# Last stage of an encoder block: the product with p split into high and low parts, and two even row tiles loaded earlier

## What is computed

```python
r = DEEPNORM_ALPHA * h + moe_ffn(h, ...)                       # 512 x 1024
r = r + jax.nn.sigmoid(r @ ple_w_gate[i]) * (p[i] @ ple_w_proj[i])   # p: 512 x 256
h = layer_norm(r, ln2_g[i], ln2_b[i])
```

## Time and profile before

| | us |
|---|---|
| median of 3 runs | 1092.02 |
| lowest and highest | 1091.96, 1093.88 |
| the profiled execution | 1090.4 |
| its span, first to last instruction | 1088.6 |
| TensorE busy | 1059.9 (97%) |
| VectorE busy | 853.4 (78%) |
| ScalarE busy | 716.7 (66%) |
| mean granted TensorE clock | 0.997 |

### The profile page before, as it was taken

One profiled execution on the slowest core, in us unless ns is written; L12 is line 12 of the kernel. 1 busy time (PEld: TensorE's weight loads), 2 busy tenths in 40 slices (PEclk: granted clock), 3 DMA queues, 4 the chain that ended last, 5 costly groups with the idle time before them and its releaser, 6 DMA issues.

```text
span 1088.6 us, 15813 instructions
## 1 busy us (share of the span) xinstructions
PE 1059.9 (97%) x5382; PEld 864.9 (79%) x5382; DVE 853.4 (78%) x906; ACT 716.7 (66%) x819; POOL 237.1 (22%) x173
## 2 busy tenths in 40 slices
PE   5999999999999999999999999999999999999996
PEld 4778877778888767888888888888888888888585
DVE  6654345663355788999999999999999999999476
ACT  3431244451242527888889988888998888888643
POOL 1000000000005120333333333333333333332101
PEclk9999999999999999999999999999999999999998
DMA  8532221214356449999999999999999999999831
GB/s 296 196 117 78 78 78 39 79 39 155 116 199 237 155 133 347 366 388 391 384 379 384 392 372 392 395 389 388 382 385 374 392 385 390 382 390 342 271 120 61
DMA packets 72571, 294.80 MB, mean 271 GB/s; under 512 B 15312, under 2 KB 18384, under 8 KB 47696
## 3 DMA queue, kind: packets, MB, share of 16 engines
q1 hardware_dynamic: 52944, 256.43, 60.0%
q0 software_dynamic: 19008, 35.71, 12.7%
q10 hardware_dynamic: 576, 2.10, 0.5%
HBM read 283.67 MB, written 44.04 MB: 301 GB/s over the span
## 4 chain that ended last, share of the span: by engine, by line
PE 92%; DMA 3%; DVE 2%; ACT 1%; issue 1%; SPq 0%; DVEq 0%; POOLq 0%; ACTq 0%
PE ps L416 26%; PE ps L418 25%; PE ps L417 25%; PE ps L1562 5%; PE ps L1586 1%; PE ps L1275 1%; PE ps L753 1%; PE ps L777 1%; PE ps L764 1%; DMA residual_rows<-y,put_idx 1%; DMA raw<-in_w_in 1%; DVE w_lo L400 1%; PE ps L325 1%; ACT w_hi L395 1%; PE ps L1546 0%
## 5 line engine op out<-in xcount | busy, mean ns | idle before, releaser
L1825 DVE TENSOR_TENSOR w_lo<-gu_raw,w_hi 128x2048 fp32r<-128x2048 f32 x128 | 292.3, 2284 | 1.0 <-ACT w_hi L1673 1.0
L1673 ACT ACTIVATE w_hi<-gu_raw 128x2048 fp32r<-128x2048 f32 x128 | 245.0, 1916 | 0.0
L416 PE MATMUL ps<-w_hi,xgT_hi 128*128 128x512 f32 x512 | 200.1, 391 | 0.8 <-issue 0.8
L418 PE MATMUL ps<-w_hi,xgT_lo 128*128 128x512 f32 x512 | 199.8, 390 | 0.0
L417 PE MATMUL ps<-w_lo,xgT_hi 128*128 128x512 f32 x512 | 199.2, 389 | 0.0
L1830 DVE TENSOR_TENSOR dn_lo<-dn_raw,dn_hi 128x2048 fp32r<-128x2048 f32 x62 | 142.2, 2293 | 20.8 <-ACT dn_hi L1682 20.8
L416 PE MATMUL ps<-w_hi,act_hi 128*128 128x512 f32 x368 | 146.6, 398 | 0.0
L418 PE MATMUL ps<-w_hi,act_lo 128*128 128x512 f32 x368 | 143.7, 390 | 0.0
L417 PE MATMUL ps<-w_lo,act_hi 128*128 128x512 f32 x368 | 143.4, 390 | 0.0
L1682 ACT ACTIVATE dn_hi<-dn_raw 128x2048 fp32r<-128x2048 f32 x62 | 118.8, 1917 | 0.0
L416 PEld LDWEIGHTS ps<-w_hi,xgT_hi 128*128 128x128 f32 x512 | 96.1, 188 | 21.3 <-issue 1.3
(11 more groups left out here) (218 smaller groups left out, 1763.6 us busy)
## 6 DMA issues: line engine op xcount, KB each, us to landing
gu_raw<-in_moe_w_gate SPq DMA_DIRECT2D x64, 1024.0 KB
gu_raw<-in_moe_w_up SPq DMA_DIRECT2D x64, 1024.0 KB
dn_raw<-in_moe_w_down SPq DMA_DIRECT2D x62, 1024.0 KB
raw<-in_w_in SPq DMA_DIRECT2D x18, 1024.0 KB, 5.2
h_rows<-x_rows SPq DMA_DIRECT2D x8, 512.0 KB, 4.5
raw<-in_w_out SPq DMA_DIRECT2D x4, 1024.0 KB, 4.9
ple_raw<-in_ple_w_gate SPq DMA_DIRECT2D x4, 1024.0 KB, 9.9
x_rows<-in_x SPq DMA_DIRECT2D x4, 512.0 KB, 10.0
```

Source lines behind the costliest of these rows:

```text
L416: nc.tensor.matmul(out, x_hi, w_hi, start=first, stop=False)
L418: return nc.tensor.matmul(out, x_lo, w_hi, start=False, stop=last)
L1673: nc.scalar.activation(m.w_hi[:, 2 * x.b + half], m.gu_raw[:, 2 * x.b + half], ACT.Copy).then_inc(gu_hi, 1)
L1825: nc.vector.tensor_tensor(m.w_lo[:, 2 * x.b + half], m.gu_raw[:, 2 * x.b + half], m.w_hi[:, 2 * x.b + half].bitcast(F32), ALU.subtract).th ...
```

## The change

- p times its weights is made with `product3` from high and low parts: `p_w_hi` (ScalarE, `split_p_weights`), `p_w_lo` and `pT_lo` (VectorE, `low_p`), `pT_hi` (ScalarE, `copy_turned_p`, which wrote `pT` before). In the last expert ScalarE does `split_p_weights` and `copy_turned_p` ahead of `scale_y` of expert 62; VectorE does `low_p` after `split_hT(63)`.
- The eight units go to banks 2, 7, 5, 6, 0, 1, 2, 7. Unit 0 waits for the first half of `pT_lo`, unit 4 for the second. `turn(0)` stands after all eight units.
- SP waits for the last scatter into `residual_rows` and loads the even rows of tiles 0 and 1; after `scattered` it loads the odd rows of tiles 0 and 1, gate weights 3, then tiles 2 and 3. The gains of the last norm are loaded once all eight units are summed.
- On ScalarE `copy_pp(0)` stands ahead of `split_hi(0)`, and the other copies move up in the same way. On VectorE `split_lo(3)` and `add_rows(1)` change places.

```diff
-        self.pT = at("pT", [P, 2, SEQ], F32, 188)
+        self.pT_hi = at("pT_hi", [P, 2, SEQ], F32R, 188)
+        self.pT_lo = at("pT_lo", [P, 2, SEQ], F32R, 184)
+        self.p_w_hi = at("p_w_hi", [P, HC], F32R, 168)
+        self.p_w_lo = at("p_w_lo", [P, HC], F32R, 192)
...
                 embedding.load_weights(sp, 2)
+                sp.wait_ge(put[0], 16 * ((r + 1) * (NE // 2) + ZEROS[0]))
+                embedding.load_even(sp, 0)
+                embedding.load_even(sp, 1)
...
                     split_hT(x)
+                    with act.If(peak[0] <= (x.r + 1) * CAP):
+                        embedding.split_p_weights(act)
+                        embedding.copy_turned_p(act)
                     scale_y(x.next(-1))
                     put_list(x)
-                    with act.If(peak[0] <= (x.r + 1) * CAP):
-                        embedding.copy_turned_p(act)
                     scale_y(x, bank=XT)
...
                     split_down(x, -1)
                     split_hT(x)
+                    with dve.If(peak[0] <= (x.r + 1) * CAP):
+                        embedding.low_p(dve)
...
+    OUT = (2, 7, 5, 6, 0, 1, 2, 7)
...
+    def load_even(self, sp, t):
+        sp.dma_start(self.m.x[:, t], self.acc[0][t * P:(t + 1) * P, :]).then_inc(self.rows_in[t], 16)
+
+    def load_odd(self, sp, t):
+        sp.dma_start(self.m.x_odd[t // 2][:, t % 2], self.acc[1][t * P:(t + 1) * P, :]).then_inc(self.rows_in[t], 16)
...
         sp.wait_ge(self.scattered, 1)
-        for t in range(NT):
-            sp.dma_start(m.x[:, t], self.acc[0][t * P:(t + 1) * P, :]).then_inc(self.rows_in[t], 16)
-            sp.dma_start(m.x_odd[t // 2][:, t % 2], self.acc[1][t * P:(t + 1) * P, :]).then_inc(self.rows_in[t], 16)
-            if t == 0:
-                self.load_weights(sp, 3)
+        self.load_odd(sp, 0)
+        self.load_odd(sp, 1)
+        self.load_weights(sp, 3)
+        for t in range(2, NT):
+            self.load_even(sp, t)
+            self.load_odd(sp, t)
+        sp.wait_ge(self.p_sum, 2 * NT)
         self.norm.load_affine(sp, self.a["ln2_g"][0], self.a["ln2_b"][0])
...
+    def split_p_weights(self, act):
+        act.wait_ge(self.pw_in, 16)
+        self.nc.scalar.activation(self.m.p_w_hi[:], self.m.p_w[:], ACT.Copy).then_inc(self.pw_hi, 1)
+
+    def low_p(self, dve):
+        m = self.m
+        dve.wait_ge(self.pw_hi, 1)
+        self.nc.vector.tensor_tensor(m.p_w_lo[:], m.p_w[:], m.p_w_hi[:].bitcast(F32), ALU.subtract).then_inc(self.pw_lo, 1)
+        for pair, bank in enumerate(self.PT):
+            cols = slice(2 * pair * P, 2 * (pair + 1) * P)
+            dve.wait_ge(self.pT_hi_done, 2)
+            self.nc.vector.tensor_tensor(m.pT_lo[:, :, cols], self.turned_p(bank), m.pT_hi[:, :, cols].bitcast(F32),
+                                         ALU.subtract).then_inc(self.pT_ready, 1)
...
-        pe.wait_ge(self.pw_in, 16)
+        pe.wait_ge(self.pw_lo, 1)
         for u in range(2 * NT):
             t, c = divmod(u, 2)
-            if u == 0:
-                pe.wait_ge(self.pT_ready, 2)
-            if u >= 2:
-                pe.wait_ge(self.p_out, u - 1)
+            if u in (0, 4):
+                pe.wait_ge(self.pT_ready, u // 4 + 1)
+            if u == 2:
+                pe.wait_ge(self.p_out, 1)
+            if u >= 6:
+                pe.wait_ge(self.p_out, u - 5)
             for j in range(2):
-                last = nc.tensor.matmul(ps[:, MAIN[c]], m.pT[:, j, t * P:(t + 1) * P],
-                                        m.p_w[:, j * D + c * 512:j * D + (c + 1) * 512],
-                                        start=(j == 0), stop=(j == 1))
+                rows, cols = slice(t * P, (t + 1) * P), slice(j * D + c * 512, j * D + (c + 1) * 512)
+                last = product3(nc, ps[:, self.OUT[u]], m.pT_hi[:, j, rows], m.pT_lo[:, j, rows],
+                                m.p_w_hi[:, cols], m.p_w_lo[:, cols], j == 0, j == 1)
             last.then_inc(self.p_sum, 1)
-            if u == 6:
-                turn(0)
+        turn(0)
...
+        copy_pp(0)
         ring.split_hi(act, 0)
-        copy_pp(0)
+        copy_pp(1)
         ring.split_hi(act, 1)
-        copy_pp(1)
         copy_pp(2)
+        copy_pp(3)
         ring.split_hi(act, 2)
-        copy_pp(3)
-        copy_pp(4)
-        copy_pp(5)
-        copy_pp(6)
+        for u in range(4, 2 * NT):
+            copy_pp(u)
         high_part(0)
-        copy_pp(7)
         ring.split_hi(act, 3)
...
         low_part(0)
+        ring.split_lo(dve, 3)
         add_rows(1)
-        ring.split_lo(dve, 3)
```

More of the change, by code:

```diff
@@ L2002, in __init__ @@
         self.p_turned, self.pT_ready, self.p_sum, self.p_out = sem("p_turned"), sem("pT_ready"), sem("p_sum"), sem("p_out")
+        self.pw_hi, self.pw_lo, self.pT_hi_done = sem("pw_hi"), sem("pw_lo"), sem("pT_hi_done")
         self.row_sum, self.turned, self.hi_done, self.lo_done = (sem("row_sum"), sem("turned"), sem("hi_done"),
@@ L2025, in load_weights @@
         self.ring.load(sp, i)
+    def load_even(self, sp, t):
+        sp.dma_start(self.m.x[:, t], self.acc[0][t * P:(t + 1) * P, :]).then_inc(self.rows_in[t], 16)
+    def load_odd(self, sp, t):
+        sp.dma_start(self.m.x_odd[t // 2][:, t % 2], self.acc[1][t * P:(t + 1) * P, :]).then_inc(self.rows_in[t], 16)
     def sync(self, sp):
-        m = self.m
         sp.wait_ge(self.scattered, 1)
-        for t in range(NT):
-            sp.dma_start(m.x[:, t], self.acc[0][t * P:(t + 1) * P, :]).then_inc(self.rows_in[t], 16)
-            sp.dma_start(m.x_odd[t // 2][:, t % 2], self.acc[1][t * P:(t + 1) * P, :]).then_inc(self.rows_in[t], 16)
-            if t == 0:
-                self.load_weights(sp, 3)
+        self.load_odd(sp, 0)
[5 more added lines that the diff above has]
+        sp.wait_ge(self.p_sum, 2 * NT)
         self.norm.load_affine(sp, self.a["ln2_g"][0], self.a["ln2_b"][0])
@@ L2053, in copy_turned_p, with turned_p @@
             act.wait_ge(self.p_turned, pair + 1)
-            self.nc.scalar.activation(self.m.pT[:, :, 2 * pair * P:2 * (pair + 1) * P],
-                                      self.ps[:, bank].rearrange("p (j n) -> p j n", n=2 * P),
-                                      ACT.Copy).then_inc(self.pT_ready, 1)
+            self.nc.scalar.activation(self.m.pT_hi[:, :, 2 * pair * P:2 * (pair + 1) * P], self.turned_p(bank),
+                                      ACT.Copy).then_inc(self.pT_hi_done, 1)
+    def turned_p(self, bank):
+        return self.ps[:, bank].rearrange("p (j n) -> p j n", n=2 * P)
+    def split_p_weights(self, act):
[10 more added lines that the diff above has]
+                                         ALU.subtract).then_inc(self.pT_ready, 1)
     def gpsimd(self, pool):
@@ L2092, in tensor @@
             if u < 2:
-                pe.wait_ge(self.p_out, 2 * NT - 1 + u)
+                pe.wait_ge(self.p_out, 5 + u)
             else:
@@ L2131, in copy_pp @@
             act.wait_ge(self.p_sum, u + 1)
-            nc.scalar.activation(m.pp[:, t, c * 512:(c + 1) * 512], ps[:, self.MAIN[c]],
+            nc.scalar.activation(m.pp[:, t, c * 512:(c + 1) * 512], ps[:, self.OUT[u]],
                                  ACT.Copy).then_inc(self.p_out, 1)
```

## The result

| | before | changed |
|---|---|---|
| median, us | 1091.99 (6 runs) | 1095.84 (6 runs) |
| lowest and highest | 1090.94, 1093.88 | 1094.73, 1096.76 |
| profiled execution, us | 1090.4 | 1095.33 |
| its span | 1088.6 | 1093.5 |
| mean granted clock over the runs | 0.9972 (beside the experiments) | 0.9947 |

The ratio is 1.0038, with a 95% interval of 1.0028 to 1.0048: 3.8 us slower (the interval is 3.1 to 5.2 us), where 1.6 were forecast. The time lies 0.3 us above the stated range.

A forecast was written before the change was run, and what follows sets the result against it. Bound by the chain from expert 63 through the last scatter and row loads to turn(0), tied with TensorE's p products. turn(0) 0.4 us late, less 0.3, then the swap's hold: turn(1) +1.6, median 1093.6, range 1091.6 to 1095.5.

The forecast's parts named there:

- The p product's 3.5 us: TensorE's products with p: 48 matmuls in 10.9 us instead of 14.4, 3.5 us less work but not on the path.
- the tie at turn(0): Before turn(0), two paths tie: the seventh p product ends at 1029.65 us, tile 0's rows are there at 1029.76.
- ScalarE's order: New copies ahead of scale_y(62) on ScalarE start it 1.55 us later and make the last scatter 1.1 us later.
- the gap of 0.30 on GpSimd: Between scatters 62 and 63 on GpSimd: 0.30 us taken, starting scatter 63 at 1019.8; with 0.72, 1020.2.
- The way from turn(0) to the end of gate unit 0: On TensorE, without unit 7's passes after the turn: 8.05 us instead of 8.35, giving back 0.3.
- the row loads: Early even loads: first takes 3.6 us, odd 0 lands at 1028.9, turn(0) only 0.4 us later than before.
- rival B: Gate weights 3 land later still, at 1035.9 with a 9.9 us load; turn(1) ends 3.5 us late, 1095.5; chance 0.25.
- the swap: split_lo(3) ahead of add_rows(1) on VectorE: TensorE waits from 1038.25 to 1039.45, turn(1) ends 1.6 us later.
- Rival A: turn(1) is not held, gate weights 3 landing by 1032.8; +0.1 to +0.4 us left, median 1092.3; chance 0.2.
- the clock at no charge: TensorE's new idle pieces of 1.5, 1.1, 1.1 and 1.2 us are too short to lower the clock; nothing charged.
- Rival D: Clock falls in the 1.5 us gap before the p products; 48 half-speed matmuls take 10.9 us more, 1102 at worst; chance 0.03.

The follow-up runs named there:

- e11: Changed kernel with old load order, swap undone, VectorE making p_w_hi, expert 62's rows scaled first, two idle pieces filled: 1091.65 us, ratio 0.9999 to the kernel before.
- e2: Changed kernel with the row loads in the old order, none issued before all scatters are done: 1093.36 us, ratio 1.0021 to the kernel before.
- e5: Changed kernel with old load order, weights of p loaded earlier and split in ScalarE's idle time, turned p copied behind put_list(63): 1092.5 us, ratio 1.0008.
- e1: Changed kernel with only VectorE's swap undone, add_rows(1) ahead of split_lo(3) again: 1095.23 us, ratio 1.0036 to the kernel before.
- e3: Changed kernel with eight extra matmuls, results overwritten, filling TensorE's wait for the first half of pT_lo: 1095.79 us, ratio 1.0048 to the kernel before.
- c1: The changed kernel itself measured and profiled once more, nothing altered: 1096.2 us, ratio 1.0035 to the kernel before.
- e6: As e5, with VectorE's swap undone and only tile 0's even rows loaded after scatter 62: 1093.67 us, ratio 1.0024 to the kernel before.

## Why the prediction was wrong, point by point

**Right: the direction and where to look.** The p product's 3.5 us were not on the path (e11: 0.9999), the tie at turn(0) was real, and ScalarE's order was what moved the scatters. That step stands nearly to the number: scatter 63 at D + 3.07 forecast, D + 3.48 and D + 2.92 in the two profiles, with the gap of 0.30 on GpSimd that I took over 0.72. Alone it costs 1.6 us. I had it at 1.1 at the scatter, and then let the early loads pay it back. The way from turn(0) to the end of gate unit 0 took 8.04 us, as forecast (8.05). But the direction came out right in part by luck: the term that made most of my 1.6 us is worth 0.2.

**Wrong, the largest step: the row loads.** I gave the first early load 3.6 us, the time of one with nothing ahead, let the queue run on at the old pace, and had odd 0 land at D + 12.2, 3.9 us after its issue. The early loads were issued about when I had them (D + 6.4 against D + 6.0), but they hardly moved before the last scatter had landed, and the first took 6.0 us. Odd 0 followed behind both at the pace of my sum and landed at D + 14.9, 6.3 us after its issue, and 6.8 in the second profile. In the old order only one load stands ahead of it, and turn(0) comes 1.3 us sooner (e2). The prediction weighed that the even loads share the engines with the last scatter, but only as an argument for rival B. Early loads are a cost and not a repayment: +1.2 us on the kernel before, 0.7 with the clock held up. Gate weights 3 stood behind them: 9.36 us where I had 8, which is near rival B's 9.9. Rival B named a load that was late, and its sum (1095.5) came out near in part by luck: its path is the one through the swap, which costs 0.2, and the clock is not in it. Rival A's estimate had gate weights 3 down at 1031.9, which is D + 15.2; they landed at D + 18.9.

**Wrong: what holds turn(1).** I made the swap the main term, 1.2 us of waiting. It would have held, had turn(0) not been 2.7 us later than I put it; as it was, both paths arrived within 0.1 us, and undoing the swap gives 0.2 with the clock held up and without. A wait that the chain names last is no price: the path beside it has to be read too.

**Wrong: the clock at no charge.** I compared idle pieces of 1.1 to 1.5 us one by one with a single row, 3.9 us of idleness at the end (the last matmul ended at 1079.0, the clock fell at about 1082.9). Here the clock fell after 1.92 us in one profile and while TensorE idled for 3.34 in another, and over all runs its mean fell by 0.0025. Rival D had the place (the gap ahead of the first product) at a chance of 0.03 and was priced as one large loss. In truth the mean was 0.993 to 0.996 in all twelve executions of the changed kernel (0.996 to 0.998 before), so the clock falls in most or all of them. Among the products of the changed kernel this costs nothing, since they still end 1.5 us ahead of turn(0) (in e5, where the rows came sooner, it cost 0.5). Where it meets gate unit 0, the way from turn(0) to turn(1) is 2.3 to 3.4 us longer (e1, e3, c1). On average over the runs the clock costs 1.1 to 1.4. The Trainium skill, "TensorE: Matmul & The Clock Gate", section on HAM oscillation, says that waits between bursts of matmuls send the clock back to half; the waits of its example are longer, about 3 to 5 us. These runs show the same behind shorter ones: the mean went from 0.9947 to 0.9975 when the idle pieces were filled.

The terms by runs: ScalarE's order 1.6, early loads 0.7 to 1.2, clock 1.1 to 1.4, swap 0.2, product and the shorter way behind turn(0) about -0.1 (0.9999). Their sum is 3.5 to 4.3, and 3.8 was measured. Each comes with an interval of about 1 us either way, so the order of the small ones isn't settled.

What stays open is the rest of the loads' delay. That the early loads hardly move before the last scatter has landed, and then both stand ahead of odd 0, would account for the first profile; no run tested it apart. But odd 0 landed 2.7 us behind the last even load in the second profile and 3.9 in e6, where the old order has 1.3 to 1.5. In the changed kernel's windows the DMA share is 1.16 at 283 GB/s from 1028 to 1030, 0.79 at 299 from 1030 to 1032, and 1.01 at 405 from 1032: the engines are first busy while little arrives, then in part idle. Whether it is the scatter, or a second start of the queue, wasn't separated.

No variant here beats the kernel before. TensorE was full there until the rows came, so work saved ahead of the rows turns into waiting, and waiting can lower the clock.

## What to carry to other kernels

Before crediting work taken off a full engine, find what else ends at the same moment: here the rows came 0.1 us after the products, and 3.5 us saved were worth nothing. New work placed on another engine ahead of a link of the critical chain is not free because that engine idles later: 1.9 us of copy and 1.1 us moved forward on ScalarE made the last scatter 1.3 us later and the kernel 1.6. A load issued while another transfer is under way isn't ahead by the time between the issues: 2.3 us of lead brought nothing here. When a change turns work into idleness on TensorE, count on the clock falling behind one of the idle pieces in some executions, and ask which products follow them; filling one piece can move the idleness to where it costs more.

## What the runs showed of the hardware

- A load of 512 KB lands 4.5 to 4.7 us after its issue behind one of the same size issued just ahead; where that one was issued 2.2 us earlier, during the last scatter, it takes 5.9 (one early load, e6), and 6.1 to 6.8 behind two (seven profiles).
- The first of these early loads, issued while the last scatter was under way, took 4.1 to 6.3 us; issued after it had landed, the first load took 3.5 to 3.8.
- With the bulk loads of the expert stage in the queue, a load issued 5.7 us earlier landed no earlier by the distance from D: it took 15.5 us (e5) against 9.5.
- A 128x2048 copy to float32r takes ScalarE 1.92 us (changed kernel) and VectorE 1.23 (e11), both from SBUF. VectorE, in its timeline of e11:

```profile
1015.88 1.23 DVE L2080 CAST p_w_hi<-p_w 128x2048 fp32r<-128x2048 f32 x1 [0.27 <-DMA p_w<-in_ple_w_proj]
```

- The granted clock fell to 1.2 GHz after idle pieces of 1.92 us (changed kernel), 2.01 (e6) and 2.17 (e5), and stayed at 2.4 in e2 with pieces of 1.88, 1.96 and 1.16 (its profile: the first third of gate unit 0 took 2.06 us there, the full pace).
